# Four projections of a gated linear attention mixer with tokens, not features, on the output partitions, turned back by transposes

## The chip, the cores and the metric

The kernel runs on one core of a Trainium2 chip. The metric is the device time in microseconds from launch to end, the median of several executions. TensorE multiplies, VectorE and ScalarE work elementwise, SyncE and ScalarE issue the transfers; each engine runs its own instruction stream in order and waits on semaphores.

## The reference

Two transformer blocks follow each other on 256 tokens of width 2048, all in float32. The change is in the second block's mixer, whose output part is this:

```python
def _gla_output(o, g, gain, w_gla_out):
    of = o.transpose(0, 2, 1, 3)
    of = of * lax.rsqrt(jnp.mean(of * of, axis=-1, keepdims=True) + RMS_EPS)
    b, l = of.shape[:2]
    of = of.reshape(b, l, D_VAL).astype(g.dtype) * gain
    return (of * jax.nn.silu(g)) @ w_gla_out

def _merge(o, g, p, bg, rows, gla_norm_gain, w_gla_out, w_pool_group, pool_scale, w_pool_out, w_out):
    y_gla = _gla_output(o, g, gla_norm_gain, w_gla_out)
    y_pool = _pool_branch(p, rows, w_pool_group, pool_scale, w_pool_out)
    gate_gla, gate_pool = jnp.split(jax.nn.sigmoid(bg), N_BRANCH, axis=-1)
    return (gate_gla * y_gla + gate_pool * y_pool) @ w_out
```

Here g (2048 wide) and bg (4096 wide) are products of the block's input with columns of w_in_2, o is the output of a chunked linear attention with 4 heads of 512 values, p is a 1024 wide pooling branch.

## The kernel before

**Split products.** Every float32 operand is cut into a high part (rounded to float32r) and a low part, and a product is x_high·w_high + x_low·w_high + x_high·w_low. Weights come in chunks of 1 MB (128 x 2048), each made of two **halves** of 128 x 1024. ScalarE writes a half's high part (line 1308, tile RH, a ring of NR = 5 halves), VectorE subtracts to get the low part (line 2198, tile RL, in place in the ring of NW = 5 chunks). A high slot is free again once TensorE has done its high products and VectorE its subtraction, so both engines stand at most 5 halves ahead. SyncE sends the next chunk when a slot's low products are done (semaphore `used`).

**Two forms of a product.** `gemm` has weight tiles (128 input rows by 128 output columns) in the array and streams the tokens: a half is 8 matmuls of 512 columns, the high and low parts of the 256 tokens side by side (line 529), and 8 of 256 columns with the low weights (line 540). The result has features on the partitions and tokens in the free dimension; its two halves must be added, ScalarE copying one out (`low_part`, line 1315, tile LT) and VectorE adding (`summed`, line 2252, or in place, 2257). A block is 256 output features, which is 4 halves for 2048 input features and 2 for 1024. With `paired=True` two halves go high, high, low, low. `gemm_n` has the token tiles in the array and streams the weights: a half is 12 matmuls of 512 columns (lines 615 and 617 with high weights, 625 with low ones), accumulated whole. The result has tokens on the partitions; a block is 512 features, 8 halves for 2048 input features. It makes v2 (attention values) and p2 (pool input).

**Order of the work.** Nothing is scheduled by a program: each engine's stream is written by generators ("lanes") whose `yield`s are steps, and `run` walks several lanes in turn. One step of a product is about one half. `slow(lane, 1.42)` stretches a lane so that each of its steps takes 1.42 steps of the product beside it; TensorE and VectorE put the beside lane ahead of the product in a step, ScalarE behind it.

The stretch in question, in halves of TensorE's count:
- for each head h of 4: `lat_head(h)` (the attention, small float32 products in lines 1117 to 1159) beside v2 of the next head (8 halves, not for h = 3) and **bg2** (16 halves, `gemm`, branch gates). A bg2 block goes VectorE sum into GB, then by a transfer of 256 KB from ScalarE's queue (line 2013) to the scratch tensor `gate` in HBM. At a head's end its output is scaled per token (line 2998, ON), turned by 8 transposes in two groups (line 1171) and copied with the gain into OT (line 3005);
- `load_gates`: ScalarE waits until all 16 gate writes have landed, then issues four reads of 512 KB (line 2021);
- **g2** (32 halves, `gemm` paired): sum, Silu, times OT, split into H high and low;
- p2 (16 halves), **gout** (32 halves, `gemm` unpaired) with the pool's small products beside its first 8, **pout** (16 halves, paired). ScalarE fetches the second half of the gates in gout (line 2060) and takes their sigmoid (line 2065);
- out2 (32 halves, paired), with H as its input, and behind it a layer norm, on which the feed-forward products wait.

Within direction d of a head, VectorE's lines 2834 and 2837 (sums of the next decay) and then 2957 and 2958 (K3, Q3) are one step; TensorE's line 1130 multiplies K3 and Q3, behind lines 1117 and 1126. `ada` is a lane of VectorE that multiplies streamed modulation weights (line 2718, 1.28 us each).

## Time and profile before

| | us |
|---|---|
| median of 3 runs (lowest, highest) | 2909.44 (2907.69, 2909.84) |
| the profiled execution's own time | 2907.68 |
| span in its profile | 2906.4 |
| TensorE busy | 2869.6 (99%) |
| VectorE busy | 2103.5 (72%) |
| ScalarE busy | 1440.4 (50%) |

A matmul's duration in the trace includes its way through the array, and matmuls overlap; the distance from start to start is what one costs. All starts are microseconds from the span's start. The stretch above runs from 1457 (first head) to 2047 (start of out2).

### The profile page before, as it was taken

To read this page: it belongs to the slowest core of one execution; us is meant where nothing else is said; L and a number is where in the kernel's file an instruction comes from. 1 tells how busy PE (TensorE), PEld (TensorE's weight loads), DVE (VectorE), ACT (ScalarE), POOL (GpSimd) and SP (SyncE) were. 2 spreads that over 40 slices of the span, in tenths; PEclk is the share of its full clock that TensorE was granted. 3 is DMA by queue.
4 is the path that set the end of the run, shared out by engine and by line. 5 is a ranking of instruction groups with operands and counts; after the bars stand their busy time and mean duration, and the time that the engine had idled before them with its cause. 6 is when DMAs were issued, how large, how long until landed. Compare 5 with 4: busy or idle time off the path is not lost.

```text
span 2906.4 us, 41107 instructions
## 1 busy us (share of the span) xinstructions
PE 2869.6 (99%) x16702; PEld 2503.3 (86%) x16702; DVE 2103.5 (72%) x2907; ACT 1440.4 (50%) x1929; POOL 11.4 (0%) x26
## 2 busy tenths in 40 slices
PE   8999999999999999999999999999999999999998
PEld 7889989888888888887888888888888888888887
DVE  6566777998999876698767665559987765555657
ACT  5455656544444444455444444544555444444444
POOL 0000000000000000000000000000000000000000
PEclk9999999999999999999999999999999999999999
DMA  7555345777777885587745555668647765555552
GB/s 273 189 197 199 131 174 207 270 270 263 269 270 262 319 304 189 202 295 264 269 174 194 183 180 196 218 259 303 242 152 286 290 221 188 188 189 189 188 190 115
DMA packets 107997, 650.97 MB, mean 224 GB/s; under 512 B 12017, under 2 KB 12273, under 8 KB 44065
## 3 DMA queue, kind: packets, MB, share of 16 engines
q1 hardware_dynamic: 100512, 623.04, 58.8%
q10 hardware_dynamic: 5328, 17.83, 1.5%
q0 software_dynamic: 1968, 7.47, 0.7%
q8 instruction: 132, 2.16, 0.3%
q14 instruction: 57, 0.46, 0.0%
HBM read 636.76 MB, written 11.53 MB: 223 GB/s over the span
## 4 chain that ended last, share of the span: by engine, by line
PE 95%; DVE 3%; ACT 1%; issue 1%; DMA 0%; SPq 0%; ACTq 0%; DVEq 0%
PE PS L529 51%; PE PS L540 27%; PE PS L615 3%; PE PS L617 3%; PE PS L625 3%; PE PS L524 1%; DVE RL L2198 1%; PE PS L526 1%; PE PS L864 1%; PE PS L1141 0%; PE PS L1155 0%; ACT RH L1308 0%; DVE X L3178 0%; PE PS L833 0%; PE PS L1072 0%
## 5 line engine op out<-in xcount | busy, mean ns | idle before, releaser
L2198 DVE TENSOR_TENSOR RL<-RW,RH 128x1024 fp32r<-128x1024 f32 x968 | 1164.2, 1221 | 425.3 <-ACT RH L1308 420.8
L1308 ACT ACTIVATE RH<-RW 128x1024 fp32r<-128x1024 f32 x968 | 1006.8, 1054 | 635.3 <-PE PS L529 492.9
L529 PE MATMUL PS<-A,RH 128*128 128x512 f32 x4272 | 1046.3, 394 | 11.6 <-ACT RH L1308 8.6
L529 PEld LDWEIGHTS PS<-A,RH 128*128 128x128 f32 x4272 | 782.5, 189 | 167.2 <-ACT RH L1308 8.9
L540 PEld LDWEIGHTS PS<-A,RL 128*128 128x128 f32 x4544 | 595.2, 191 | 28.4
L540 PE MATMUL PS<-A,RL 128*128 128x256 f32 x4544 | 607.0, 283 | 0.0
L529 PE MATMUL PS<-H,RH 128*128 128x512 f32 x2248 | 542.8, 392 | 0.0
L529 PEld LDWEIGHTS PS<-H,RH 128*128 128x128 f32 x2248 | 412.5, 188 | 80.3 <-issue 0.8
L1315 ACT ACTIVATE LT<-PS 128x512 f32<-128x512 f32 x214 | 127.7, 597 | 474.3 <-PE PS L540 474.2
L540 PEld LDWEIGHTS PS<-H,RL 128*128 128x128 f32 x2304 | 297.7, 191 | 12.4
L540 PE MATMUL PS<-H,RL 128*128 128x256 f32 x2304 | 302.8, 283 | 0.0
L2252 DVE TENSOR_TENSOR G<-PS,LT 128x512 f32<-128x512 f32 x115 | 79.3, 690 | 124.5 <-ACT LT L1315 116.8
L615 PE MATMUL PS<-RH,A 128*128 128x512 f32 x416 | 163.4, 393 | 0.0
L617 PE MATMUL PS<-RH,A 128*128 128x512 f32 x416 | 162.2, 390 | 0.0
L625 PE MATMUL PS<-RL,A 128*128 128x512 f32 x416 | 111.2, 389 | 0.0
L2718 DVE CUSTOM_DVE_ANT_0 G<-G,MODT 128x1024 f32<-128x1024 f32 x80 | 102.4, 1280 | 0.2
L2718 DVE CUSTOM_DVE_ANT_0 G<-G,C 128x1024 f32<-128x1024 f32 x80 | 102.4, 1280 | 0.1
L615 PEld LDWEIGHTS PS<-RH,A 128*128 128x128 f32 x416 | 78.1, 188 | 18.9 <-issue 2.9
L625 PEld LDWEIGHTS PS<-RL,A 128*128 128x128 f32 x416 | 78.1, 188 | 16.3
L617 PEld LDWEIGHTS PS<-RH,A 128*128 128x128 f32 x416 | 78.2, 188 | 15.8
L3169 DVE SCALAR_TENSOR_TENSOR X<-LT,MODT,X 128x256 f32<-128x256 f32 x60 | 26.4, 482 | 51.3 <-ACT LT L1315 49.0
L524 PE MATMUL PS<-A,RH 128*128 128x256 f32 x240 | 60.7, 291 | 0.0
(280 smaller groups left out, 1734.7 us busy)
## 6 DMA issues: line engine op xcount, KB each, us to landing
RW<-in_w_fin SPq DMA_DIRECT2D x88, 1024.0 KB, 4.8
G<-in_w_ada SPq DMA_DIRECT2D x160, 512.0 KB, 6.2
RW<-in_w_up SPq DMA_DIRECT2D x64, 1024.0 KB, 4.9
RW<-in_w_down SPq DMA_DIRECT2D x64, 1024.0 KB, 4.9
RW<-in_w_fout SPq DMA_DIRECT2D x44, 1024.0 KB, 4.8
RW<-in_w_v SPq DMA_DIRECT2D x32, 1024.0 KB, 4.8
RW<-in_w_bg SPq DMA_DIRECT2D x32, 1024.0 KB, 4.8
RW<-in_w_k SPq DMA_DIRECT2D x16, 1024.0 KB, 5.5
```

The costliest lines, as they stand in the source:

```text
L524: t.matmul(pair[mm][:, 0:256], w, x2(4 * c + k)[1], start=c == 0 and k == 0, stop=False, skip_group_check=True)
L526: done = t.matmul(pair[mm][:, 0:256], w, x2(4 * c + k)[2], start=False, stop=False, skip_group_check=True)
L529: done = t.matmul(pair[mm][:, :], w, x2(4 * c + k)[0], start=c == 0 and k == 0, stop=False, skip_group_check=True)
L540: done = t.matmul(pair[mm][:, 0:256], wl[:, k, mm * 128:mm * 128 + 128], x2(4 * c + k)[1], start=False, stop=c == halves - 1 and k == 3, s ...
L615: t.matmul(out[mm], hi(2 * c + k)[:, rows[mm]], wh[:, k, :], start=first and k == 0, stop=False, skip_group_check=True)
L617: done = t.matmul(out[mm], lo(2 * c + k)[:, rows[mm]], wh[:, k, :], start=False, stop=False, skip_group_check=True)
L625: done = t.matmul(out[mm], hi(2 * c + k)[:, rows[mm]], wl[:, k, :], start=False, stop=last and k == 1, skip_group_check=True)
L1308: a.activation(m.high(x), m.slot(j)[:, x % 2 * HC:x % 2 * HC + HC], ACT.Copy).then_inc(s["hi"], 1)
L1315: a.activation(pair2(m.LT[g % 2]), m.sum_l[g % 2], ACT.Copy).then_inc(s["lt"], 1)
L2198: v.tensor_tensor(m.low(x), m.slot(j)[:, x % 2 * HC:x % 2 * HC + HC], m.high(x).bitcast(F32), ALU.subtract).then_inc(s["lo"], 1)
L2252: v.tensor_tensor(pair2(out), m.sum_h[g % 2], pair2(m.LT[g % 2]), ALU.add).then_inc(m.pair[g % 2], 1)
L2718: v.tensor_tensor_reduce(slot if which == whiches - 1 else m.products, slot, m.silu_row[cb][:, k:k + 1024], 1.0, begin_with, ALU.mult, ALU ...
```

## The change

bg2, g2, gout and pout go from `gemm` to `gemm_n`, with their weights laid out by rows in HBM. Where the result was wanted with features on partitions (the input of gout, from g2, and of out2, from pout) it is turned by transposes on TensorE, 128 x 128 each, in groups of 4 (`turn`), three halves into the next block for g2 and two for pout; ScalarE and VectorE then take high and low parts from PSUM. The attention's output stays with tokens on the partitions, so its 8 transposes a head go. bg2 no longer passes VectorE: ScalarE copies both PSUM banks of a block one after the other through the one buffer GB, and waits in its own stream for the first write to land before the second copy. `lat_head` has 17 steps for 19 and is stretched by 1.58 for 1.42. out2 runs its first four halves unpaired (`single=4`).

TensorE: `gemm_n` takes the halves of a block and a lane beside it.
```diff
-    def gemm_n(blocks, hi, lo, need):
-
+    def gemm_n(blocks, hi, lo, need, halves=8, beside=None):
+
+        rest = None
...
-            for c in range(8):
+            for c in range(halves):
...
+                first, last = c == 0, c == halves - 1
                 out = [m.banks[2 * (g % 2) + mm][:, :] for mm in range(2)]
                 rows = [slice(mm * 128, mm * 128 + 128) for mm in range(2)]
                 for mm in range(2):
@@ -625,7 +627,12 @@
                         done = t.matmul(out[mm], hi(2 * c + k)[:, rows[mm]], wl[:, k, :], start=False,
                                         stop=last and k == 1, skip_group_check=True)
                 done.then_inc(s["used"], 1)
-                yield
+                if rest is not None:
+                    next(rest, None)
+                yield
+            if beside is not None:
+                rest = num.later = beside(b)
+                next(rest, None)
             if b + 1 < blocks:
```

TensorE's transposes and who waits for them, and the new products:

```diff
-        for j in range(2):
-            bk = banks.next()
-            wait_empty(bk)
-            for k in range(2):
-                for i in range(2):
-                    f = (2 * j + k) * 128
-                    t.wait_ge(ob[i].empty, ob[i].n)
-                    done = t.transpose(bk.ap[:, k * 256 + i * 128:k * 256 + i * 128 + 128], m.ON[i][:, f:f + 128], ident)
-            done.then_inc(bk.full, 1)
-            yield
-
...
+    def turn(b, j, ready):
+
+        bk = banks.next()
+        wait_empty(bk)
+        t.wait_ge(ready, 2 * b + 2)
+        for k in range(2):
+            for i in range(2):
+                f = (2 * j + k) * 128
+                done = t.transpose(bk.ap[:, k * 256 + i * 128:k * 256 + i * 128 + 128], m.gt[b % 2][i][:, f:f + 128], ident)
+        done.then_inc(bk.full, 1)
+        num.turned.append(bk)
...
+    def turned_of(first):
+
+        def need(c):
+            bk = num.turned[first + c]
+            t.wait_ge(bk.empty, bk.n)
+        return need
...
-    L.bg2 = lambda: gemm(4, 4, A2, nothing)
+    L.bg2 = lambda: gemm_n(2, hA, lA, nothing)
...
-    L.g2 = lambda: gemm(8, 4, A2, nothing, paired=True)
-    L.gout = lambda: gemm(8, 4, H2, lambda c: t.wait_ge(s["gl"], c + 1))
-    L.pout = lambda: gemm(8, 2, A2, lambda c: t.wait_ge(s["pl"], c + 1), paired=True)
+    def g2():
+        def beside(b):
+            yield
+            yield
+            yield
+            for j in range(2):
+                turn(b, j, s["gmul"])
+                yield
+        yield from gemm_n(4, hA, lA, nothing, beside=beside)
+
+    def pout():
+        def beside(b):
+            yield
+            yield
+            for j in range(2):
+                turn(b, j, s["mr"])
+        yield from gemm_n(4, hA, lA, lambda c: t.wait_ge(s["pl"], c + 1), halves=4, beside=beside)
...
+    L.gout = lambda: gemm_n(4, m.H.high, m.H.low, turned_of(0))
...
-    L.out2 = lambda: gemm(8, 4, H2, lambda c: t.wait_ge(s["ml2"], 17 + c), beside=normed(0), paired=True,
-                          whole=(7,))
+    L.out2 = lambda: gemm(8, 4, H2, turned_of(8), beside=normed(0), paired=True,
+                          whole=(7,), single=4)
```

ScalarE: the branch gates and g2.

```diff
         def evac(b, g):
-            n, i = divmod(num.kept, 2)
-            num.kept += 1
-            yield
-            yield
-            a.wait_ge(m.pair[g % 2], g // 2 + 1)
-            a.dma_start(io["gate"][n][:, i * 512:i * 512 + 512], m.GB).then_inc(l["kept"], 16)
-            yield
-        yield from gemm(4, 4, evac, late=True)
+            a.wait_ge(s["used"], num.half)
+            for i in range(2):
+                if num.kept:
+                    a.wait_ge(l["kept"], 16 * num.kept)
+                copy = a.activation(m.GB, m.banks[2 * (g % 2) + i][:, :], ACT.Copy)
+                if i == 0:
+                    copy.then_inc(s["gb"], 1)
+                    a.wait_ge(s["gb"], num.kept // 2 + 1)
+                else:
+                    copy.then_inc(m.pair[g % 2], 1)
+                    evacuated(g)
+                a.dma_start(io["gate"][num.kept // 2][:, i * 512:i * 512 + 512], m.GB).then_inc(l["kept"], 16)
+                num.kept += 1
+                yield
+                yield
+        yield from gemm_n(2, evac)
...
     def load_gates():
         a.wait_ge(l["kept"], 16 * num.kept)
-        a.wait_ge(num.on.full, num.on.filled)
+        for bk in num.ob:
+            a.wait_ge(bk.empty, bk.n)
...
-            a.wait_ge(m.pair[g % 2], g // 2 + 1)
-            a.activation(m.tm2[b % 3], m.tm2[b % 3], ACT.Silu).then_inc(s["g_a"], 1)
-            yield
-            a.wait_ge(s["gmul"], b + 1)
-            a.activation(m.H.high(2 * b, 2), pair2(m.tm2[b % 3]), ACT.Copy).then_inc(s["gh"], 1)
-        yield from gemm(8, 4, evac)
+            a.wait_ge(s["used"], num.half)
+            for i in range(2):
+                r = a.activation(m.gt[b % 2][i], m.banks[2 * (g % 2) + i][:, :], ACT.Silu)
+            r.then_inc(m.pair[g % 2], 1)
+            yield
+            yield
+            yield
+            yield
+            for j in range(2):
+                bk = banks.next()
+                a.wait_ge(bk.full, bk.filled)
+                for k in range(2):
+                    kt = 4 * b + 2 * j + k
+                    r = a.activation(m.H.high(kt), bk.ap[:, k * 256:k * 256 + 256], ACT.Copy, scale=m.par("gla_gain", kt))
+                r.then_inc(s["gh"], 1)
+                yield
+        yield from gemm_n(4, evac, late=True)
```

VectorE: the end of a head, g2 and pout (bg2's own part is gone).

```diff
-            v.tensor_scalar(m.ON[i], ob[i].ap[:, :], m.SM[:, 30 + i:31 + i], None, ALU.mult).then_inc(ob[i].empty, 1)
-        yield
-        for j in range(2):
-            bk = banks.next()
-            v.wait_ge(bk.full, bk.filled)
-            for k in range(2):
-                ft = 4 * h + 2 * j + k
-                r = v.tensor_scalar(m.OT[:, ft * 256:ft * 256 + 256], bk.ap[:, k * 256:k * 256 + 256],
-                                    m.par("gla_gain", ft), None, ALU.mult)
-            r.then_inc(bk.empty, 1)
-            num.on_t = num.ot = bk
-            yield
+            at_i = 2048 * i + 512 * h
+            v.tensor_scalar(m.OT[:, at_i:at_i + 512], ob[i].ap[:, :], m.SM[:, 30 + i:31 + i], None,
+                            ALU.mult).then_inc(ob[i].empty, 1)
...
+    L.bg2 = lambda: gemm_n(2, nothing)
...
-
-        def evac(b, g):
-            tm, d = m.tm2[b % 3], slice(512 * b, 512 * b + 512)
-            summed(tm, g)
-            v.wait_ge(s["g_a"], b + 1)
-            v.tensor_tensor(tm, tm, m.OT[:, d], ALU.mult).then_inc(s["gmul"], 1)
-            yield
-            v.wait_ge(s["gh"], b + 1)
-            v.tensor_tensor(m.H.low(2 * b, 2), pair2(tm), m.H.high(2 * b, 2).bitcast(F32), ALU.subtract).then_inc(s["gl"], 1)
-        yield from gemm(8, 4, evac)
+            yield
+            evacuated(g)
+            for i in range(2):
+                tm, at_i = m.gt[b % 2][i], 2048 * i + 512 * b
+                v.tensor_tensor(tm, tm, m.OT[:, at_i:at_i + 512], ALU.mult).then_inc(s["gmul"], 1)
+            yield
+            yield
+            yield
+            yield
+            for j in range(2):
+                bk = banks.next()
+                v.wait_ge(s["gh"], 2 * b + j + 1)
+                for k in range(2):
+                    kt = 4 * b + 2 * j + k
+                    r = v.scalar_tensor_tensor(m.H.low(kt), bk.ap[:, k * 256:k * 256 + 256], m.par("gla_gain", kt),
+                                               m.H.high(kt).bitcast(F32), ALU.mult, ALU.subtract)
+                r.then_inc(bk.empty, 1)
+                yield
+        yield from gemm_n(4, evac, late=True)
...
-            stepped(v.tensor_tensor(tm, tm, m.gate_b(2 * b, 2), ALU.mult))
-            wait_step()
-            v.tensor_tensor(tm, tm, m.gate_a(2 * b, 2), ALU.add).then_inc(s["mr"], 1)
-            yield
-            v.wait_ge(s["mh2"], 16 + b + 1)
-            v.tensor_tensor(m.H.low(2 * b, 2), pair2(tm), m.H.high(2 * b, 2).bitcast(F32), ALU.subtract).then_inc(s["ml2"], 1)
-        yield from gemm(8, 2, evac)
+            for i in range(2):
+                r = v.tensor_tensor(m.gt[b % 2][i], m.banks[2 * (g % 2) + i][:, :], m.gate_b(4 * b, 4)[:, 512 * i:512 * i + 512],
+                                    ALU.mult)
+            r.then_inc(m.pair[g % 2], 1)
+            evacuated(g)
+            for i in range(2):
+                tm = m.gt[b % 2][i]
+                v.tensor_tensor(tm, tm, m.gate_a(4 * b, 4)[:, 512 * i:512 * i + 512], ALU.add).then_inc(s["mr"], 1)
+            yield
+            yield
+            yield
+            for j in range(2):
+                bk = banks.next()
+                v.wait_ge(s["mh2"], 16 + 2 * b + j + 1)
```

The order of the lanes:

```diff
-        run(*L.beside(slow(L.lat_head(h), 1.0 if h == 3 else 1.42), chain(idle() if h == 3 else L.v2(), L.bg2())))
+        run(*L.beside(slow(L.lat_head(h), 1.0 if h == 3 else 1.58), chain(idle() if h == 3 else L.v2(), L.bg2())))
...
-    run(chain(L.p2(), both(after(1, L.pool()), L.gout()), L.pout()), L.cp_loads(), beside=beside)
-    run(L.out2(), beside=beside)
+    run(chain(L.p2(), both(after(1, L.pool()), L.gout()), L.pout()), L.cp_loads(), L.later(), beside=beside)
+    run(*L.beside(L.later(), L.out2()), beside=beside)
```

**What moves in the order.** ScalarE, at the end of the last head's bg2, before (2013 writes a block, 2021 reads the gates, 1308 makes the first high part that is not ready by then, the fifth half of g2):

```order
L1998 ACTIVATE SM<-SM 128x2 [waits s_on_a]
L1315 ACTIVATE LT<-PS 128x512 [waits s_used]
L2013 DMA gate<-G 128x512 [waits s_pair1]
L2021 DMA G<-gate 128x1024 [waits s_full7,l_kept]
L2021 DMA G<-gate 128x1024 x3
L1308 ACTIVATE RH<-RW 128x1024 [waits s_hused,s_lo,l_w0]
```

and after the change (2046 the copies, 2053 the writes, 2064 the reads, 1343 the high part):

```order
L2033 ACTIVATE SM<-SM 128x2 [waits s_on_a]
L2046 ACTIVATE G<-PS 128x512 [waits l_kept,s_used]
L2053 DMA gate<-G 128x512 [waits s_gb]
L2046 ACTIVATE G<-PS 128x512 [waits l_kept]
L2053 DMA gate<-G 128x512 [waits s_pair1]
L2064 DMA G<-gate 128x1024 [waits s_empty5,s_empty4,l_kept]
L2064 DMA G<-gate 128x1024 x3
L1343 ACTIVATE RH<-RW 128x1024 [waits s_hused,s_lo,l_w0]
```

Two copies and two writes stand where there were one copy and one write, and the second copy waits on `l_kept`, the landing of the first write.

VectorE, second direction of the third head, before (2198 is the low part of a half, 2834 and 2837 the decay sums, 2957 and 2958 make K3 and Q3):

```order
L2198 TENSOR_TENSOR RL<-RW,RH 128x1024 [waits s_hi]
L2834 SCALAR_TENSOR_TENSOR G<-G 128x512 [waits s_d_ln]
L2837 SCALAR_TENSOR_TENSOR G<-G 128x512 [waits s_d_z]
L2957 COPY G<-G 128x2x64 [waits s_kb,s_et]
L2958 TENSOR_TENSOR G<-G,SM 128x2x64
L2957 COPY G<-G 128x2x64 [waits s_qa]
L2958 TENSOR_TENSOR G<-G,SM 128x2x64
```

and after (2256 is the low part, 3017 and 3018 make K3 and Q3):

```order
L2256 TENSOR_TENSOR RL<-RW,RH 128x1024 [waits s_hi] x2
L2895 SCALAR_TENSOR_TENSOR G<-G 128x512 [waits s_d_ln]
L2898 SCALAR_TENSOR_TENSOR G<-G 128x512 [waits s_d_z]
L3017 COPY G<-G 128x2x64 [waits s_kb,s_et]
L3018 TENSOR_TENSOR G<-G,SM 128x2x64
L3017 COPY G<-G 128x2x64 [waits s_qa]
L3018 TENSOR_TENSOR G<-G,SM 128x2x64
```

Counted through the program, the last low part ahead of K3 was that of half 553, and is that of half 555 after the change; TensorE's product of K3 and Q3 stands ahead of half 552 in both.

TensorE, from the last low products of pout into out2, after the change (627 pout, 530 and 541 out2's high and low products, 1180 the transposes):

```order
L627 MATMUL PS<-RL,A 128x512 x3
L530 MATMUL PS<-H,RH 128x512 [waits s_empty4,s_hi,s_pair0]
L530 MATMUL PS<-H,RH 128x512 x3
L530 MATMUL PS<-H,RH 128x512 [waits s_empty5]
L530 MATMUL PS<-H,RH 128x512 x3
L541 MATMUL PS<-H,RL 128x256 [waits s_lo]
L541 MATMUL PS<-H,RL 128x256 x7
L1180 MATMUL PS<-C,G 128x128 [waits s_mr,s_empty6]
L1180 MATMUL PS<-C,G 128x128 x3
L1180 MATMUL PS<-C,G 128x128 [waits s_mr,s_empty7]
L1180 MATMUL PS<-C,G 128x128 x3
```

The last eight transposes stand behind one half of out2 and wait for `s_mr`, VectorE's additions; before there was nothing between the halves.

## Rows read from the trace of the kernel before

**Rows 1.** The page: the chain that ended last, share of the span by engine.
```profile
PE 95%; DVE 3%; ACT 1%; issue 1%; DMA 0%; SPq 0%; ACTq 0%; DVEq 0%
```

**Rows 2.** Windows: us; busy us (x) of PE, PEld, DVE, ACT, POOL; clock, DMA, GB/s.
```profile
1570.19:1586.95 16.76, 16.76 (x98) 14.75 (x97) 13.18 (x19) 8.94 (x12) 0.00 (x0) 1.00 0.48 168
1766.97:1856.12 89.15, 89.15 (x516) 78.82 (x515) 53.70 (x58) 44.80 (x55) 0.00 (x0) 1.00 0.59 215
1856.12:1899.66 43.54, 43.54 (x194) 36.04 (x193) 22.43 (x21) 23.96 (x25) 2.11 (x4) 1.00 0.66 242
1938.64:2002.89 64.25, 64.25 (x371) 56.55 (x369) 56.06 (x72) 30.79 (x33) 0.00 (x0) 1.00 0.92 352
2002.89:2047.42 44.53, 44.53 (x258) 39.34 (x257) 39.37 (x49) 24.52 (x31) 0.00 (x0) 1.00 0.61 224
```

**Rows 3.** Timeline of TensorE, third head: start us, us, line, operation.
```profile
1697.32 2.00 PE L529 MATMUL PS<-A,RH 128*128 128x512 f32 x8
1699.16 1.11 PE L540 MATMUL PS<-A,RL 128*128 128x256 f32 x8
1700.11 0.60 PE L1171 MATMUL PS<-C,G 128*128 128x128 f32 x4
1700.46 2.09 PE L529 MATMUL PS<-A,RH 128*128 128x512 f32 x8
1702.39 1.12 PE L540 MATMUL PS<-A,RL 128*128 128x256 f32 x8
```

**Rows 4.** The same, around the small products in a half of values.
```profile
1640.65 0.39 PE L615 MATMUL PS<-RH,A 128*128 128x512 f32 x1
1642.46 1.07 PE L625 MATMUL PS<-RL,A 128*128 128x512 f32 x4
1645.14 0.48 PE L615 MATMUL PS<-RH,A 128*128 128x512 f32 x1
1647.08 1.07 PE L625 MATMUL PS<-RL,A 128*128 128x512 f32 x4
```

**Rows 5.** Timeline of ScalarE, then SyncE, where the last branch gate product ends.
```profile
1766.38 0.60 ACT L1315 ACTIVATE LT<-PS 128x512 f32<-128x512 f32 x1 [2.30 <-PE PS L540]
1768.32 0.33 ACTq L2013 DMA_DIRECT2D gate<-G  x1
1772.08 1.78 ACTq L2021 DMA_DIRECT2D G<-gate  x4
...
1766.37 0.33 SPq L3349 DMA_DIRECT2D RW<-in_w_g  x1
```

**Rows 6.** Line 2013, all 16 gate writes: time from issue to landing.
```profile
DMA to landing us min/median/max: 2.0/3.7/4.7
```

**Rows 7.** Timeline of ScalarE, then VectorE: a high part, and the low part behind it.
```profile
1642.72 1.06 ACT L1308 ACTIVATE RH<-RW 128x1024 fp32r<-128x1024 f32 x1 [1.64 <-PE PS L617]
1643.81 1.23 DVE L2198 TENSOR_TENSOR RL<-RW,RH 128x1024 fp32r<-128x1024 f32 x1
```

**Rows 8.** Timeline of VectorE, second direction of the third head.
```profile
1665.91 1.22 DVE L2198 TENSOR_TENSOR RL<-RW,RH 128x1024 fp32r<-128x1024 f32 x1
1669.37 0.28 DVE L2958 TENSOR_TENSOR G<-G,SM 128x128 f32<-128x128 f32 x1
```

**Rows 9.** Timeline of TensorE behind it.
```profile
1671.94 1.11 PE L540 MATMUL PS<-A,RL 128*128 128x256 f32 x8
1674.19 0.71 PE L1130 MATMUL PS<-G 128*128 128x128 f32 x4
```

**Rows 10.** Timeline of VectorE at the end of the pool output product.
```profile
2050.33 0.69 DVE L3086 TENSOR_TENSOR G<-G 128x512 f32<-128x512 f32 x1
```

**Rows 11.** Timeline of ScalarE where the pool gates return; landing of those reads.
```profile
1951.58 1.06 ACT L2065 ACTIVATE G<-G 128x1024 f32<-128x1024 f32 x1 [9.59 <-DMA G<-gate]
DMA to landing us min/median/max: 6.8/8.9/13.1
```

**Rows 12.** Window in the norm behind the last product of the mixer.
```profile
2143.70:2150.60 6.90, 5.80 (x14) 4.58 (x15) 6.59 (x16) 4.42 (x9) 0.00 (x0) 0.51 0.01 2
```

More of the change, by code:

```diff
@@ L436, in __init__ @@
         self.ST = self.ON[0]
+        self.gt = [[G[:, E0 + 1024 * p + 512 * i:E0 + 1024 * p + 512 * i + 512] for i in range(2)] for p in range(2)]
         self.tm2 = [G[:, E0 + 512 * i:E0 + 512 + 512 * i] for i in range(3)]
@@ L503, in block_begins, with gemm @@
             t.wait_ge(m.pair[g % 2], g // 2)
-    def gemm(blocks, halves, x2, need, zipped=False, beside=None, paired=False, whole=(), by_tile=None):
+    def gemm(blocks, halves, x2, need, zipped=False, beside=None, paired=False, whole=(), by_tile=None, single=0):
         rest, g0 = None, num.block
@@ L1342, in gemm, with gemm_n @@
             yield
-    def gemm_n(blocks, evac):
+    def gemm_n(blocks, evac, halves=8, late=False):
         rest = None
@@ L1348, in gemm_n @@
             num.block += 1
-            for c in range(8):
+            for c in range(halves):
                 prepare(num.half)
@@ L1354, in gemm_n @@
                 yield
-            rest = evac(b, g)
+            if rest is not None:
+                exhaust(rest)
+            rest = num.later = evac(b, g)
             next(rest, None)
@@ L1358, in gemm_n @@
                 yield
-        exhaust(rest)
+        if not late:
+            exhaust(rest)
         if not num.tight:
@@ L2068, in gout @@
     def gout():
-        yield from gemm(8, 4, nothing)
+        yield from gemm_n(4, nothing)
         num.y_used = num.half
@@ L2074, in evac @@
             yield
+            yield
             a.wait_ge(s["used"], num.y_used)
-            a.wait_ge(s["mr"], b + 1)
-            a.activation(m.H.high(2 * b, 2), pair2(m.tm2[(16 + b) % 3]), ACT.Copy).then_inc(s["mh2"], 1)
-        yield from gemm(8, 2, evac)
+            for j in range(2):
+                bk = banks.next()
+                a.wait_ge(bk.full, bk.filled)
+                a.activation(m.H.high(4 * b + 2 * j, 2), pair2(bk.ap), ACT.Copy).then_inc(s["mh2"], 1)
+        yield from gemm_n(4, evac, halves=4, late=True)
     L.g2, L.p2, L.pool, L.gout, L.pout = g2, p2, pool, gout, pout
@@ L2222, in gemm, with gemm_n @@
             yield
-    def gemm_n(blocks, evac):
+    def gemm_n(blocks, evac, halves=8, late=False):
         rest = None
@@ L2228, in gemm_n @@
             num.block += 1
-            for c in range(8):
+            for c in range(halves):
                 prepare(num.half)
@@ L2234, in gemm_n @@
                 yield
-            rest = evac(b, g)
+            if rest is not None:
+                exhaust(rest)
+            rest = num.later = evac(b, g)
             next(rest, None)
@@ L2238, in gemm_n @@
                 yield
-        exhaust(rest)
+        if not late:
+            exhaust(rest)
         if not num.tight:
@@ L3011, in vector_program @@
-    L.lat_head = lat_head
-    num.kept = 0
-    def bg2():
-        def evac(b, g):
-            if num.kept:
-                v.wait_ge(l["kept"], 16 * num.kept)
-            num.kept += 1
-            summed(m.GB, g)
-            yield
-        yield from gemm(4, 4, evac)
-    L.bg2 = bg2
+    L.lat_head = lat_head
+    L.bg2 = lambda: gemm_n(2, nothing)
+    L.later = lambda: num.later
     L.load_gates = lambda: None
     def g2():
-        v.wait_ge(num.ot.empty, num.ot.n)
+        for bk in num.ob:
+            v.wait_ge(bk.empty, bk.n)
@@ L3364, in gemm, with gemm_n @@
             yield
-    def gemm_n(blocks):
+    def gemm_n(blocks, halves=8):
         for b in range(blocks):
-            for c in range(8):
+            for c in range(halves):
                 next_half()
@@ L3505, in sync_program @@
     L.zero = L.heads_begin = L.heads_end = L.load_gates = nothing
-    L.lat_head = lambda h: idle(19)
-    L.bg2 = lambda: gemm(4, 4)
-    L.g2 = L.gout = L.out2 = lambda: gemm(8, 4)
+    L.lat_head = lambda h: idle(17)
+    L.bg2 = lambda: gemm_n(2)
+    L.g2 = L.gout = lambda: gemm_n(4)
+    L.out2 = lambda: gemm(8, 4)
+    L.later = idle
     def p2():
@@ L3515, in sync_program @@
     L.pool = lambda: idle(15)
-    L.pout = lambda: gemm(8, 2)
+    L.pout = lambda: gemm_n(4, 4)
     L.cp_loads = lambda: idle(12)
```

51 lines of the change are left out of this document (26 added, 25 removed).

## Prediction

> **What bounds the kernel now.** I read the page's chain first: TensorE carries 95% of it [rows 1]. Then windows over the stretch that changes: in each of the five TensorE's busy time equals the window, and the granted clock is 1.00, its 2.4 GHz level [rows 2]. So nothing done on VectorE or ScalarE is worth anything here until TensorE waits for it; what counts is how long TensorE's own stream is, and whether the new order makes it wait. The same windows price a half of each form. bg2: 16.76 us for 6 halves, 2.793. g2, paired: 89.15 for 32, 2.786. p2, the only `gemm_n` among them: 43.54 for 16, 2.721. gout behind the pool: 64.25 for 23, 2.793. pout, paired: 44.53 for 16, 2.783. Both forms stream 6144 columns a half; `gemm_n` does it in 12 matmuls, `gemm` in 16.
>
> **The halves.** bg2 64 x (2.793 - 2.721) = 4.6 us less; g2 32 x 0.065 = 2.1; gout 32 x 0.072 = 2.3; pout 16 x 0.062 = 1.0. Together -10.0. All of it is on the path. The four unpaired halves of out2 cost 4 x (2.793 - 2.783), 0.04.
>
> Here a page of the Trainium skill speaks against the change. "TensorE: Matmul & The Clock Gate", section "Back-to-back issue gap", gives an isolated gap of N/2.4 + 2.5 ns for N columns. By it a half would be 8 x 215.8 + 8 x 109.2 ns = 2.600 us in one form and 12 x 215.8 = 2.590 in the other, and the halves would give 144 x 0.01 = 1.4 us instead of 10.0. The windows of this case decide for 2.793 and 2.721 [rows 2].
>
> **The transposes.** A group of four in a head costs what it adds between two starts of low products: 1702.39 - 1700.11 = 2.28 us with it, 1699.16 - 1697.32 = 1.84 for the high products alone, so 0.44 [rows 3]. Eight groups go: -3.5. Sixteen come. The group itself is 0.35 [rows 3]; ahead of `gemm_n`'s high products I add what these lose behind foreign work, 1647.08 - 1645.14 = 1.94 against 1642.46 - 1640.65 = 1.81, so 0.13 [rows 4]. g2: 8 x 0.48 = 3.8; pout, two groups at a time: 4 x (0.70 + 0.13) = 3.3. Net +3.6. A float32 transpose of another tile has the same shape, so both bounds are narrow: 0.35 and 0.48 a group.
>
> **What leaves VectorE and ScalarE.** The sums of two halves, the copies LT and the gain copies go; per 512 features g2 and pout have fewer instructions than before. Worth nothing: the engines were covered by TensorE, and are more so now.
>
> **New waits.** Three places, none in the trace of before.
>
> (a) End of the last bg2. ScalarE is at most four halves ahead, so TensorE can go on for 4 x 2.721 = 10.9 us after bg2's end E. ScalarE's stream there: its copy begins 0.2 after E, at the moment the next weight chunk is sent [rows 5]; 0.65 to the issue of the write; landing 3.76, as for the write at 1768.32, which also ran beside a weight chunk [rows 5]; second copy and issue 0.65; landing 3.76 again, since a second chunk is sent two halves after the first; reads of the gates and restart 1.9 (1.78 for the issues, 0.1 behind them) [rows 5]; one high part 1.06 [rows 7]; 0.1 for the semaphore. Ready at E + 12.1: a wait of **1.2 us**. Queued behind the waiting instruction are all of g2's high parts from the fifth half on, and TensorE waits for them. The write lands in 2.0 to 4.7 us over its 16 issues [rows 6]: bounds 0 and 3.1 us. I keep the value near 3.7, the median and the row of the same place. At the ends of the other three heads ScalarE stops only for one landing and has no reads: ready at about E + 6.8, so covered.
>
> Of this a second page gives a shorter price. "DMA: Bandwidth & Descriptors", section "Anatomy of one DMA — SWDGE (gpsimd) path", has 2.0 us plus bytes/436 GB/s: an estimate of 2.6 us for 256 KB. By it the wait would be gone and the sum 1.2 us lower.
>
> (b) K3 and Q3 of the second direction, in three heads. With the stretch of 1.58 VectorE makes them behind the low part of half n+3 instead of n+1, n being the half in front of which TensorE wants them. Let s be the start of the low products of half n-2. The high part starts at s + 0.26 (1642.72 against 1642.46) and its low part 1.09 later [rows 4, 7]; from there to the last copy's end it is 1669.65 - 1665.91 = 3.74 [rows 8]: s + 5.1. TensorE reaches line 1130 at s + 0.91 + 2.72 and then 1.30 for the small products ahead (2.25 in the trace from the low products on, less 0.95 for those) [rows 9]: s + 4.9. Wait **0.2 a head, 0.6 in all**; bounds 0 and one half each, 8 us.
>
> (c) Out2's first transposes. VectorE needs two multiplications and two additions of 0.7 each from pout's end [rows 10], so 3.0 with 0.2 to begin; TensorE has one half, 2.79, in between. Wait **0.3**; bounds 0 and 1.6, if one of the modulation products (1.3 us) stands in front.
>
> **Sum.** -10.0 + 0.04 + 3.6 + 1.2 + 0.6 + 0.3 = **-4.2 us**. The profiled execution took 2907.68, so it would take 2903.5. The median of the runs shown is 1.8 above it; on that I put 2909.44 - 4.2 = 2905.2. Behind out2 nothing changes but the moment: in the norm the clock was granted at 0.51 for 6.9 us with TensorE busy for 5.8 [rows 12]; if that stretch falls otherwise by a half, it is 1.5 us either way.
>
> **Rivals.**
> 1. The waits don't come: landings of 2 to 3 us, the head's steps in time. Then -6.3, 2903.1. For it: the low end of [rows 6]; against it: the write at this very place.
> 2. Slower: ScalarE's stop at the landings. At each of the four bg2 ends it stands still for a landing, at the last for two. Beside the reads of the pool gates a transfer took up to 13.1 us and ScalarE waited 9.59 [rows 11]. At 13.1 a head end would be ready at E + 16.2, 5.3 us late, three times, and the last at E + 30.8, 19.9 late: about +31, 2940. It decides from a landing of some 9 us on. Against it: no gate write took over 4.7 [rows 6].
> 3. The heads run late by a whole half: 2.7 us each at K3 or at the output's products, three times: -4.2 - 0.6 + 8.1 = +3.3, 2912.7. For it: the margin in (b) is nil.
> 4. The form is worth little, as by the gap above: -1.4 + 3.6 + 2.1 = +4.3, 2913.7. By [rows 2] the form in p2 has all of its gain, beside the same engines' work. That the change doesn't do what it says would look the same; its order does show 12 matmuls a half in all four products.
>
> **Numbers.** 0.2% is 5.8 us, about what a measurement of this kernel can tell from no change. Forecast 0.62, rival 1 0.24, rival 2 0.04, rival 3 0.07, rival 4 0.03. Faster by over 5.8: 0.15 of rival 1 and 0.05 of the forecast with the clock's 1.5 us: 0.20. Slower: rival 2 and a part of 3 and 4: 0.07. Same: 0.73. The likeliest case's own range is 2902 to 2908; with rival 1 below and rival 3 above I give 2901.5 to 2911.5.
>
> **What would show it.** Windows of the new g2 and of pout: 2.72 us a half plus 0.48 or 0.42 a group of transposes. TensorE's wait for a high part once, 10.9 us after bg2's end, of about 1 us; for K3 or Q3 three times under 0.5; for an addition once at out2. Gate writes landing in about 3.7. The prediction is wrong if a half of g2 isn't 2.72, if waits in the stretch sum to over 6 us, or if the norm behind it changes by more than 2 us.

## The result, and the profile after

The changed kernel takes **2919.51 us** (median of 5 runs, 2918.15 to 2921.15) where the kernel before takes 2909.44: the ratio is 1.0037, 95% interval 1.0026 to 1.0048. The forecast was 2905.2 and no change, in a range up to 2911.5: the kernel is slower, by 10.1 us. The profiled execution is the median one, 11.8 us over that of before; 1.0 of this stood there before the first head.

The page after: span, busy times, the chain by engine [rows 1], and one group of the new form.

```profile
span 2918.2 us, 39902 instructions
PE 2869.7 (98%) x16158; PEld 2478.5 (85%) x16158; DVE 2069.7 (71%) x2859; ACT 1430.6 (49%) x1913; POOL 11.4 (0%) x26
...
PE 92%; DVE 4%; ACT 1%; DMA 1%; issue 1%; ACTq 0%; SPq 0%; DVEq 0%
...
L617 PE MATMUL PS<-RH,A 128*128 128x512 f32 x864 | 345.7, 400 | 4.0 <-ACT RH L1343 4.0
```

TensorE has 544 matmuls less and is busy as long as before; VectorE and ScalarE do less. The chain, which was 95% TensorE, now has 3 points less of it, and a gate write (DMA) in it. Line 617's group shows 4.0 us of idle TensorE in front of a `gemm_n` product, ended by a high part of ScalarE; the page of before has nothing idle in front of that form. The same engine's waits, from the first head to the norm (waited for; us in total, times, longest):

```profile
PE PS L530 <- DVE A L3282: 4.1, 3, 2.2
PE PS L1137 <- DVE G L3018: 4.1, 3, 2.9
PE PS L617 <- ACT RH L1343: 4.0, 1, 4.0
PE PS L557 <- DVE A L3282: 3.4, 1, 3.4
PE PS L1180 <- DVE G L3076: 1.7, 1, 1.7
PE PS L1180 <- DVE G L3147: 0.9, 1, 0.9
PE PS L1133 <- DVE G L2929: 0.4, 1, 0.4
```

Lines 530 and 557 are the norm's, 7.5 us in all where before had 6.4. The other five are new: K3 and Q3 (1137, and 1133 ahead of it), a high part behind bg2 (617), and two groups of transposes (1180). Windows show what followed the two longest waits, and a block of g2 without either (us; busy PE, PEld, DVE, ACT, POOL; clock, DMA, GB/s):

```profile
1807.65:1826.81 19.16, 19.16 (x87) 15.81 (x86) 11.26 (x13) 8.78 (x12) 0.00 (x0) 1.00 0.52 185
1722.10:1728.90 6.80, 6.21 (x17) 5.05 (x18) 5.80 (x18) 1.06 (x1) 0.00 (x0) 0.50 0.00 0
1783.50:1786.90 3.40, 3.40 (x9) 2.66 (x10) 3.40 (x4) 3.40 (x4) 0.00 (x0) 0.50 1.01 414
```

The first is 7 halves behind a group of transposes: 19.16 - 0.13 = 7 x 2.719, the half that was forecast. The other two ran at a granted clock of 0.50, the 1.2 GHz level; eight high products took 3.56 and 3.43 there, against 1.94 and 1.81.

**Head 4.** The timeline of ScalarE from the end of the third head's bg2 on (start us, us, line, operation, idle before and who ended it):

```profile
1703.68 0.60 ACT L2046 ACTIVATE G<-PS 128x512 f32<-128x512 f32 x1 [2.18 <-PE PS L627]
1704.31 0.33 ACTq L2053 DMA_DIRECT2D gate<-G  x1
1709.71 0.60 ACT L2046 ACTIVATE G<-PS 128x512 f32<-128x512 f32 x1 [5.44 <-DMA gate<-G]
1710.34 0.33 ACTq L2053 DMA_DIRECT2D gate<-G  x1
1710.79 1.06 ACT L1343 ACTIVATE RH<-RW 128x1024 fp32r<-128x1024 f32 x1 [0.48 <-ACT G L2046]
1711.76 0.62 ACT L2000 ACTIVATE G<-G 128x512 f32<-128x512 f32 x1
```

Its two gate writes, from issue to landing:

```profile
DMA to landing us min/median/max: 5.4/5.5/5.7
```

And the timeline of VectorE, where K3 and Q3 of that head begin and end:

```profile
1721.90 0.20 DVE L3017 COPY G<-G 128x128 f32<-128x128 f32 x1
1722.36 0.28 DVE L3018 TENSOR_TENSOR G<-G,SM 128x128 f32<-128x128 f32 x1
```

Line 2000 is the head's first exponential. It started 8.2 us behind the head's first products on TensorE (1703.57); before the change it was 2.9 (1709.6 against 1706.67). K3 begins 10.14 us behind it (10.15 before the change). TensorE stood at line 1137 from 1719.78 to 1722.69.

**Behind bg2.** The same engine, where the last bg2 ends (1768.32):

```profile
1768.51 0.60 ACT L2046 ACTIVATE G<-PS 128x512 f32<-128x512 f32 x1 [2.18 <-PE PS L627]
1769.14 0.33 ACTq L2053 DMA_DIRECT2D gate<-G  x1
1774.53 0.60 ACT L2046 ACTIVATE G<-PS 128x512 f32<-128x512 f32 x1 [5.42 <-DMA gate<-G]
1775.16 0.33 ACTq L2053 DMA_DIRECT2D gate<-G  x1
1780.12 1.97 ACTq L2064 DMA_DIRECT2D G<-gate  x4
1782.22 2.01 ACT L1343 ACTIVATE RH<-RW 128x1024 fp32r<-128x1024 f32 x2 [7.09 <-issue]
```

Each step is as forecast except the two landings: 5.4 and 4.9 us, not 3.76 twice. Ready at 15.0 behind the end, not 12.1.

**The transposes of g2's last block.** The timeline of ScalarE, and under it that of VectorE:

```profile
1864.30 1.09 ACT L2072 ACTIVATE G<-PS 128x512 f32<-128x512 f32 x2 [2.51 <-PE PS L627]
1865.41 1.28 ACT L2094 ACT_TABLE_LOAD   x1
1866.70 3.90 ACT L2094 ACTIVATE G<-G 128x1024 f32<-128x1024 f32 x4
1870.51 3.88 ACT L1343 ACTIVATE RH<-RW 128x1024 fp32r<-128x1024 f32 x4
```

```profile
1871.58 1.22 DVE L2256 TENSOR_TENSOR RL<-RW,RH 128x1024 fp32r<-128x1024 f32 x1 [8.53 <-ACT RH L1343]
1872.73 1.28 DVE L3076 TENSOR_TENSOR G<-G 128x512 f32<-128x512 f32 x2
```

The four gate sigmoids stand ahead of the next high part; VectorE's low part waits for that, and the product with the attention's output, which the transposes need, stands behind the low part.

Times of TensorE at five marks (the start of what follows a half's low products, at the same count of halves), less those of before, counted from the first head; E is the end of the last bg2. The last four columns are kernels of the next section.

| | after | e1 | e4 | e9 | e11 |
|---|---|---|---|---|---|
| E | +1.2 | -6.4 | -6.5 | -6.4 | -2.4 |
| g2's end | +7.0 | -6.0 | -5.9 | +0.3 | -2.4 |
| p2's end | +9.9 | -3.1 | -5.0 | +1.2 | -1.4 |
| gout's end | +7.6 | -5.4 | -7.2 | -1.1 | -3.7 |
| out2's end | +11.3 | -1.7 | -3.5 | +2.7 | 0.0 |

### The profile page after: what moved, and what is told of

Its sections match the earlier page's. It is cut to its first block, busy times and chain, and to the rows that moved or that the text cites. A ratio compares the mean times of both kernels' runs of the same rounds, so it can differ in the third digit from the quotient of the medians.

```text
span 2918.2 us, 39902 instructions
## 1 busy us (share of the span) xinstructions
PE 2869.7 (98%) x16158; PEld 2478.5 (85%) x16158; DVE 2069.7 (71%) x2859; ACT 1430.6 (49%) x1913; POOL 11.4 (0%) x26
## 4 chain that ended last, share of the span: by engine, by line
PE 92%; DVE 4%; ACT 1%; DMA 1%; issue 1%; ACTq 0%; SPq 0%; DVEq 0%
PE PS L530 42%; PE PS L541 23%; PE PS L617 7%; PE PS L619 7%; PE PS L627 7%; DVE RL L2256 1%; PE PS L525 1%; DMA gate<-G 1%; PE PS L527 1%; ACT RH L1343 1%; PE PS L871 1%; PE PS L1148 0%; PE PS L1162 0%; DVE X L3242 0%; PE PS L840 0%
## 5 line engine op out<-in xcount | busy, mean ns | idle before, releaser
L530 PE MATMUL PS<-A,RH 128*128 128x512 f32 x3376 | 823.8, 394 | 13.6 <-ACT RH L1343 9.6
L530 PEld LDWEIGHTS PS<-A,RH 128*128 128x128 f32 x3376 | 620.3, 189 | 136.2 <-ACT RH L1343 9.9
L541 PEld LDWEIGHTS PS<-A,RL 128*128 128x128 f32 x3648 | 475.9, 191 | 21.4
L541 PE MATMUL PS<-A,RL 128*128 128x256 f32 x3648 | 485.7, 283 | 0.0
L530 PE MATMUL PS<-H,RH 128*128 128x512 f32 x1992 | 477.6, 391 | 0.0
L617 PE MATMUL PS<-RH,A 128*128 128x512 f32 x864 | 345.7, 400 | 4.0 <-ACT RH L1343 4.0
L619 PE MATMUL PS<-RH,A 128*128 128x512 f32 x864 | 339.6, 393 | 0.0
L627 PE MATMUL PS<-RL,A 128*128 128x512 f32 x864 | 232.1, 390 | 0.0
L617 PEld LDWEIGHTS PS<-RH,A 128*128 128x128 f32 x864 | 163.7, 189 | 42.8 <-ACT RH L1343 6.1
L619 PEld LDWEIGHTS PS<-RH,A 128*128 128x128 f32 x864 | 163.9, 190 | 33.9 <-issue 1.0
L627 PEld LDWEIGHTS PS<-RL,A 128*128 128x128 f32 x864 | 163.2, 189 | 34.4
L617 PE MATMUL PS<-RH,H 128*128 128x512 f32 x160 | 64.5, 403 | 0.0
```

Of the source, the lines that this page charges most:

```text
L530: done = t.matmul(pair[mm][:, :], w, x2(4 * c + k)[0], start=c == 0 and k == 0, stop=False, skip_group_check=True)
L541: done = t.matmul(pair[mm][:, 0:256], wl[:, k, mm * 128:mm * 128 + 128], x2(4 * c + k)[1], start=False, stop=c == halves - 1 and k == 3, s ...
L617: t.matmul(out[mm], hi(2 * c + k)[:, rows[mm]], wh[:, k, :], start=first and k == 0, stop=False, skip_group_check=True)
L619: done = t.matmul(out[mm], lo(2 * c + k)[:, rows[mm]], wh[:, k, :], start=False, stop=False, skip_group_check=True)
L627: done = t.matmul(out[mm], hi(2 * c + k)[:, rows[mm]], wl[:, k, :], start=False, stop=last and k == 1, skip_group_check=True)
```

## The experiments

All were timed in 5 rounds beside the kernel before on the same chip. Its median was 2908.6 to 2908.8 there, so these kernels are compared with each other to some tenths; beside the changed kernel's 2919.51 it was 2909.44, so a difference to that kernel can be 0.8 us too large or too small. Each trace is of one execution.

| | median us | ratio to before, 95% interval |
|---|---|---|
| e1_two_buffers | 2906.66 | 0.9995 (0.9986, 1.0004) |
| e2_pace | 2915.74 | 1.0025 (1.0015, 1.0035) |
| e3_two_buffers_pace | 2906.20 | 0.9993 (0.9985, 1.0002) |
| e4_sigmoids_later | 2905.12 | 0.9989 (0.9980, 0.9998) |
| e5_write_later | 2916.74 | 1.0028 (1.0016, 1.0040) |
| e6_ada | 2904.66 | 0.9986 (0.9977, 0.9995) |
| e7_ada_pace | 2904.20 | 0.9984 (0.9975, 0.9993) |
| e8_turned_twice | 2911.93 | 1.0011 (1.0002, 1.0020) |
| e9_last_block_one_buffer | 2910.98 | 1.0008 (0.9999, 1.0017) |
| e10_two_high_parts_ahead | 2916.26 | 1.0026 (1.0016, 1.0035) |
| e11_bg2_columns | 2908.40 | 0.9999 (0.9990, 1.0007) |

**e1_two_buffers.**
```diff
-                if num.kept:
+                buf = m.LT[0] if i else m.GB
+                if num.kept and i == 0:
                     a.wait_ge(l["kept"], 16 * num.kept)
-                copy = a.activation(m.GB, m.banks[2 * (g % 2) + i][:, :], ACT.Copy)
+                copy = a.activation(buf, m.banks[2 * (g % 2) + i][:, :], ACT.Copy)
...
-                a.dma_start(io["gate"][num.kept // 2][:, i * 512:i * 512 + 512], m.GB).then_inc(l["kept"], 16)
+                a.dma_start(io["gate"][num.kept // 2][:, i * 512:i * 512 + 512], buf).then_inc(l["kept"], 16)
```


> The changed kernel with the second bank of a gate block copied into a buffer of its own (the first LT tile, idle here), so that ScalarE no longer stands at the landing of the first write. Changed kernel: 2919.5 us; its profile has TensorE waiting 4.1 us for a high part behind bg2 and 4.3 us for K3 or Q3 of the first direction of heads 2 to 4 (1.0, 0.3, 2.9), with some 4.0 us more lost at the lower clock behind the two longest. Theory A, the landings (5.3 us each, the write being issued just behind a weight chunk) delay ScalarE's own steps of the head and the gate reads: all of these go, 12.4 us less, about 2907. Theory B, the heads are late because the lane is stretched by 1.58 and has no slack, whatever ScalarE does: only the wait behind bg2 and its clock go, 5.7 us less, about 2914, and the K3/Q3 waits stay as they are. Both leave the 0.2 us waits of the second direction and the waits for transposes.

2906.66, 12.9 us less. The timeline of ScalarE at the same place, and under it TensorE's waits:

```profile
1701.95 0.60 ACT L2047 ACTIVATE G<-PS 128x512 f32<-128x512 f32 x1 [2.18 <-PE PS L627]
1702.95 0.60 ACT L2047 ACTIVATE LT<-PS 128x512 f32<-128x512 f32 x1 [0.40 <-ACT G L2047]
1704.99 0.62 ACT L2000 ACTIVATE G<-G 128x512 f32<-128x512 f32 x1
```

```profile
PE PS L557 <- DVE A L3283: 3.4, 1, 3.4
PE PS L530 <- DVE A L3283: 2.9, 2, 2.3
PE PS L1180 <- DVE G L3077: 1.7, 1, 1.7
PE PS L1180 <- DVE G L3148: 0.9, 1, 0.9
```

Line 2000 is 3.2 us behind the head's first products (1701.84), K3 10.15 behind it, and TensorE no longer waits for it; the clock stays at 1.00 from the first head to the norm. Theory A holds, B falls. In the first-direction parts the start-to-start distances beyond the plain ones had been 1.0, 0.3 and 3.45 us, in the last head 2.9 more at the lower clock: 7.65, and the table has 7.6 at E. Behind bg2 it was 4.1 and 1.7.

**e2_pace** and **e3_two_buffers_pace.**
```diff
-        run(*L.beside(slow(L.lat_head(h), 1.0 if h == 3 else 1.58), chain(idle() if h == 3 else L.v2(), L.bg2())))
+        run(*L.beside(slow(L.lat_head(h), 1.0 if h == 3 else 1.42), chain(idle() if h == 3 else L.v2(), L.bg2())))
```


> The changed kernel with the stretch of the head's lane back at 1.42 (from 1.58), nothing else. Theory B (the stretch makes the heads late): the K3/Q3 waits of heads 1 to 3 go, 0.6 us in the second direction and 1.3 in the first, about 2917.5; the last head is not stretched in either and its 2.9 us wait stays. Theory A (ScalarE's stop at the landings): the second direction's 0.6 us go, the first direction's 1.3 stay or grow, since the head's steps now stand nearer to the stop: 2918.9 or more. The wait behind bg2 stays at 4.1 in both.

> Second buffer and stretch 1.42 together. Theory A: as with the second buffer alone, and 0.6 us less for the second direction: about 2906.5. If the two are independent, the difference to the second buffer alone equals that of the stretch alone to the changed kernel. A new wait at the head's end products would show that 1.58 was needed to keep the head clear of something.

e2 took 3.8 us less than the changed kernel, more than either theory said. The waits in the other heads' first direction went too, which speaks for B in part: the stop makes the head late, and the slower lane had taken the slack that would have hidden it there. The last head, not stretched, still waited 2.9 us, yet the clock did not fall behind that wait, which by itself is 2.9 of the difference. Behind bg2 it fell for 6.8 us where the changed kernel has 3.4, which takes 0.9 back. With the second buffer the stretch is worth 0.5 us (0.7 at E in the trace: 0.21 a head in the second direction, three times).

**e4_sigmoids_later** (with the second buffer).
```diff
-        for i in range(4):
-            o = m.gate_a(4 * i, 4)
-            a.activation(o, o, ACT.Sigmoid).then_inc(s["ga"], 1)
-        yield from gemm_n(2, nothing)
+        for x, _ in enumerate(gemm_n(2, nothing)):
+            if 4 <= x < 8:
+                o = m.gate_a(4 * (x - 4), 4)
+                a.activation(o, o, ACT.Sigmoid).then_inc(s["ga"], 1)
+            yield
```


> Second buffer, stretch 1.58, and the four sigmoids of the first gates (1.04 us each on ScalarE, now in a row at the start of p2) one a step from p2's fifth half on. Theory C: the 1.9 us that TensorE waited before the transposes of g2's last block came from them (VectorE's low part waited for ScalarE's high part behind the sigmoids, and the product with the attention's output stood behind that low part): the wait goes, 1.9 us less than with the second buffer alone, about 2905. Theory D: the transposes of the last block are late because the Silu and the product come at the block's end as in the other blocks, plus VectorE's own work: the wait stays at 1 us or more.

1.5 us less than e1, and the wait at g2's last transposes is gone (p2's end in the table: -5.0 for -3.1). Theory C.

**e5_write_later** and **e10_two_high_parts_ahead** (one buffer; the edit is e10's, e5 has one `prepare`).
```diff
-            a.wait_ge(s["used"], num.half)
+            used = num.half
+            if b == 1 and num.kept < 14:
+                prepare(used)
+                prepare(used + 1)
+            a.wait_ge(s["used"], used)
```


> The changed kernel, one buffer as it is, with one high part moved on ScalarE from behind the two gate copies to ahead of them, at the ends of the first three heads only (three instructions in all). The first copy then waits for TensorE's next high products: the write is issued some 3.6 us after bg2's end, 3.4 behind the weight chunk instead of 0.6. Theory A (a write lands some 6 us after the chunk it follows, and ScalarE's stop for it delays the head behind): these first writes land in 2.0 to 2.7 us instead of 5.4, the stop shrinks from 9 to under 4 us, the waits for K3/Q3 of the first direction (4.3 us, 2.4 more at the lower clock) go, about 2913; the wait behind the last bg2 stays at 4.1 to 4.4. Rival E (the landing takes some 5 us wherever it is issued, since ScalarE's queue is slow beside the weights): the stop stays, the heads are later still: 2920 or more.

> The changed kernel, one buffer as it is, with two high parts (not one) moved ahead of the gate copies at the ends of the first three heads. One high part had found its slot free and moved the write by 0.1 us only; the second has to wait for TensorE, so the write should be issued 3 to 5 us behind the chunk. Theory A (a write lands some 6 us after the issue of the chunk in front): those writes land in 2.0 to 3.3 us (5.3 in the changed kernel), ScalarE stops for under 4 us, the waits for K3 or Q3 of the first direction (4.3 us in the changed kernel, 3.5 with one high part moved) fall under 1 us, 2913 to 2915; the wait behind the last bg2 stays. Rival E (a landing takes some 5 us wherever it is issued): landings above 4.5, the waits stay, 2917 or more.

e5 missed its aim: the high part found its slot free, the write at head 4 went out at 1703.95, 0.76 behind the chunk, and landed in 5.3 us. It tells nothing of the landing. It took 2.8 us less than the changed kernel: line 2000 came 7.65 us behind head 4's first products instead of 8.19, TensorE waited 2.2 us, and in the profiled execution the clock did not fall behind that. In e10 the write goes out 4.31 us behind the chunk, at all three heads; the timeline of ScalarE at head 4, and under it that write's landing:

```profile
1704.98 1.06 ACT L1343 ACTIVATE RH<-RW 128x1024 fp32r<-128x1024 f32 x1 [2.49 <-PE PS L619]
1706.56 0.33 ACTq L2057 DMA_DIRECT2D gate<-G  x1
1708.58 0.60 ACT L2050 ACTIVATE G<-PS 128x512 f32<-128x512 f32 x1 [2.06 <-DMA gate<-G]
1710.07 0.63 ACT L2000 ACTIVATE G<-G 128x512 f32<-128x512 f32 x1 [0.89 <-ACT G L2050]
```

```profile
DMA to landing us min/median/max: 2.0/2.0/2.0
```

2.0 us, three times of three: theory A's mechanism, rival E falls. The time followed only in part: 2916.3, 3.3 less than the changed kernel, below rival E's 2917 and above theory A's 2913 to 2915. The waits of heads 2 and 3 went, and the clock fell for 3.4 us in head 4 instead of 6.8. But the copy had waited for TensorE itself, so that line 2000 comes 7.92 us behind head 4's first products and TensorE still waits 2.5 us. A shorter landing bought with a later start gains little; the stop has to go. The four traces with one buffer and that of e1 agree on this: in head 4 line 2000 at 3.15, 7.65, 7.92, 8.19 and 8.25 us behind the first products (e1, e5, e10, the changed kernel, e2) goes with waits of 0, 2.2, 2.5, 2.9 and 2.9 us.

**e6_ada** and **e7_ada_pace** (both with the second buffer and the later sigmoids; e7 with the stretch of 1.42 as well; the edit is shown against e4).
```diff
-    beside = when(L, L.ada((3,), (((20, 1.45), (1, 19.0), (11, 2.5)),)))
+    beside = when(L, L.ada((3,), (((20, 1.45), (1, 20.0), (11, 2.5)),)))
```


> Second buffer, sigmoids one a step (2905.1), and the pause of the modulation products in gout made one step longer (20.0 for 19.0), which takes the 1.28 us product out from in front of pout's last multiplications. Theory: out2's first transposes waited 1.1 us for the sums behind that product: the wait goes, 1.0 us less, about 2904. Rival: the sums are late by VectorE's low parts as well, 0.5 us or more of the wait stays; or the products' later end reaches into the norm, which then waits longer: no gain.

The wait stayed at 0.9. VectorE of e6 at pout's end:

```profile
2041.56 1.27 DVE L2781 CUSTOM_DVE_ANT_0 AF<-AF,G,MODT 128x1024 f32<-128x1024 f32 x1
2042.76 1.22 DVE L2258 TENSOR_TENSOR RL<-RW,RH 128x1024 fp32r<-128x1024 f32 x1
2043.90 1.28 DVE L3143 TENSOR_TENSOR G<-PS,G 128x512 f32<-128x512 f32 x2
2045.21 1.29 DVE L3149 TENSOR_TENSOR G<-G 128x512 f32<-128x512 f32 x2
```

The modulation product stands one place further ahead and a low part in its old place, in front of the sums: the rival. By the traces e6 is no earlier than e4 at out2's end (-3.2 for -3.5). The 0.5 us of the medians is within what the intervals leave open.

> The parts that helped together: second buffer, sigmoids one a step, the pause 20.0 (2904.7), and the stretch of 1.42. If the stretch is worth what it was beside the second buffer, 0.5 us, then about 2904.2; if the gains of heads without waits are nil, 2904.7. Both are under the kernel before, by 0.14 to 0.16%.

2904.20, the best: 4.6 us under before, and below it with its interval.

**e8_turned_twice** (against e4).
```diff
-        for k in range(2):
+        for k in (0, 1, 0, 1):
```


> As the kernel with the second buffer and the sigmoids one a step (2905.1), each of the 16 groups of four transposes issued twice into the same bank. By the prediction's price of a group, 0.35 us of its own, the 64 added transposes cost 16 x 0.35 = 5.6 us: 2910.7. Rival: the price is 0.48, with the slower start of the high products behind them: 7.7, 2912.8. If the transposes were hidden in slack of TensorE, nothing.

6.8 us more, 0.43 a group: between the two prices. In pout two groups run from 2028.83 to 2030.50 for 16 transposes, where the 8 of the changed kernel took 2039.61 to 2040.40: 1.67 against 0.79, so an added group is 0.44, while a single one shows 0.35 and pushes the rest into the high products behind it. No slack hides transposes here.

**e9_last_block_one_buffer** (against e4).
```diff
-                buf = m.LT[0] if i else m.GB
-                if num.kept and i == 0:
+                buf = m.LT[0] if i and num.kept < 15 else m.GB
+                if num.kept and (i == 0 or num.kept == 15):
```


> As the kernel with the second buffer and the sigmoids one a step (2905.1), the stop at the first write's landing put back for the last gate block alone. Theory A: the wait for a high part behind bg2 is back at some 4 us (0.3 now), and TensorE restarts at its lower clock (3.4 to 6.8 us of it, 1.6 to 2.5 us lost): 5.5 to 6.5 us more, about 2911. Rival: the lower clock of the changed kernel came from its earlier wait at the last head, not from this one: the clock stays at 1.00 and only 3.9 us are added, 2909.

5.9 us more than e4. One line of TensorE's waits, and under it the window behind that wait:

```profile
PE PS L617 <- ACT RH L1343: 3.7, 1, 3.7
```

```profile
1774.10:1780.90 6.80, 5.70 (x13) 4.45 (x14) 5.62 (x5) 5.90 (x6) 0.00 (x0) 0.50 0.98 402
```

This wait brings the lower clock without an earlier one in the last head. By the start-to-start times the first high and low products behind it took 3.58 and 1.71 us, where 1.81 and 0.91 are plain: 2.6 us on top of the wait.

**e11_bg2_columns** (with the later sigmoids). TensorE, ScalarE, VectorE and SyncE get bg2 in the form of before, with GB alone as there. The kernel leaves out what would turn these gates: they enter with features on the partitions where the other branch has tokens, so it tells of time alone.
```diff
-    L.bg2 = lambda: gemm_n(2, hA, lA, nothing)
+    L.bg2 = lambda: gemm(4, 4, A2, nothing)
```


> As the kernel with the second buffer and the sigmoids one a step (2905.1), with bg2 alone taken back to the form with weight tiles in the array and its sums on VectorE and ScalarE as before the change (the gates then enter with features on the partitions, where the other branch has tokens). The prediction's term: 64 halves x (2.793 - 2.721) = 4.6 us more, less the 0.3 to 0.5 us that TensorE waits behind bg2: about 2909.4. Rival F (the form is worth little, by the gap that the page gives 0.6 us for 64 halves): 2905.5.

3.3 us more than e4; at E 4.1 (-2.4 for -6.5). At E both have the second direction's waits, 0.14 us a head by the trace of e4 and 0.03 by that of e11, so the form is worth 4.1 us and a few tenths, some nine tenths of the term. Behind bg2 e4 waits for a high part (0.3 us) and e11 does not, which gives part of it back. Rival F falls, and with it the gap of the page "TensorE: Matmul & The Clock Gate" of the Trainium skill, section "Back-to-back issue gap", as a measure of this difference: the estimate from it was 0.01 us a half, where 4.1 us over 64 halves is 0.064.

## Why the prediction was wrong, point by point

1. **The halves, right.** 2.719 us in a new block for 2.721; gout gained 2.3 for 2.3 (p2's end to gout's end in the table), bg2 at least 4.1 for 4.6 (e11).
2. **The transposes, nearly right.** 0.48 a group in g2 as forecast, 0.91 for two in pout against 0.83. The eight that went were forecast at -3.5. Six of them stand ahead of E, where e11, with bg2 in its old form, is at -2.4; the last two stood behind E, at 0.79 us. Together 3.2. The timeline of TensorE before, from E to the start of g2:

```profile
1766.18 1.03 PE L1171 MATMUL PS<-C,G 128*128 128x128 f32 x8
1766.97 2.31 PE L529 MATMUL PS<-A,RH 128*128 128x512 f32 x9
```

3. **The landing, the step that failed first.** "landing 3.76, as for the write at 1768.32, which also ran beside a weight chunk", took the same place for the same distance. That write was issued 1.95 us behind its chunk [rows 5]; the new copy needs no sum and comes 0.63 behind. In the changed kernel all nine writes that go out 0.6 to 0.8 us behind a chunk land in 5.2 to 7.0; before, those 1.4 to 2.4 behind landed in 3.7 to 4.7, and those nearly 4 behind in 2.0 to 2.7. [Rows 6] showed the spread, not what it hung on, and its upper end 4.7 was no bound. The page "DMA: Bandwidth & Descriptors" of the Trainium skill, section "Anatomy of one DMA — SWDGE (gpsimd) path", gave an estimate of 2.6; its figures are for transfers on the GpSimd path, and these writes go out from ScalarE's queue. The estimate is off further where a chunk is in front, and high where none is (2.0). This made the wait behind bg2 4.1 for 1.2.
4. **"At the ends of the other three heads ... ready at about E + 6.8, so covered": the step that cost most.** It checked the stop against the high parts alone, of which four halves were made. Behind the stop stood also the next head's own steps, and they have no such lead: 4.75 us in the first direction, and 2.9 at the lower clock. The second direction's (b) was right, 0.21 for 0.2 a head. Rival 2 named this stop but priced it by the same high parts ("decides from a landing of some 9 us on", where the prediction's own terms make a head's end late from 10.9 - 6.8 + 3.76 = 7.9 on); at 5.4 it had decided already. Its upper bound of 13.1 is the landing of the pool gates' reads themselves [rows 11], 512 KB each, not of a transfer beside them.
5. **No term for the clock.** After the two long waits TensorE ran at 0.50 for 6.8 and 3.4 us: 4.6 us. [Rows 12] had shown a norm's wait followed by this; the prediction applied it there alone.
6. **"Worth nothing: the engines were covered by TensorE, and are more so now."** True of what left them, not of the order that remained: the sigmoids in front of p2's high parts held g2's last product, 1.9 us, which no term had.
7. **(c) out2's transposes**, 1.1 for 0.3, inside its bounds and for the reason named, one other instruction of VectorE in front.

The sum: -4.2 forecast; 2.9 for (a), 4.75 for the first direction, 4.6 for the clock, 1.9 for g2's last transposes and 0.8 for (c) make 15.0 more, +10.8, against +11.3 at the end of out2; bg2 and the eight groups together gave 0.3 to 0.8 less than forecast, which covers the rest. Without the stop at the landing (e1) the kernel is 1.9 us under before in the same call, where the forecast was 4.2: "no change" and the range would have held, with g2's last transposes (1.9) still unforeseen in it.

## What to carry to other kernels

When a change makes an in-order engine wait, list everything that it issues behind the wait and check each item's own slack: the deepest prefetch queue is the last to run dry. Price a transfer by a row with the same distance to the transfer in front of it, not by one from the same place. And a wait of 3 to 4 us on a saturated TensorE cost 1.7 to 2.9 us more where the clock fell behind it. A second buffer of 256 KB was worth 12.9 us here, more than the change of form was forecast to give (10.0).
